# A two-layer hybrid attention and convolution backbone: GpSimd issues the shifted z copies and tap loads, adaLN weights in whole units

## What is computed

```
mod = silu(c) @ w_ada[l] + b_ada[l]          # 1024 x 6144, and the same for c_ctx
sh1, sc1, gt1, sh2, sc2, gt2 = split(mod, 6)
h = rmsnorm(x, g_mix) * (1 + sc1) + sh1      # the context tokens with their own mod
q, k, v, u = split(h @ w_in)                 # 512, 128, 128, 1024 columns
a  = windowed attention (q, k, v), rotary, a sink logit per head
z  = u[:, :512] * sigmoid(u[:, 512:])
cv = silu(layernorm(depthwise_conv31(z) + b_dw))
x += gt1 * (concat(rmsnorm(a), rmsnorm(cv)) @ w_out)
x += gt2 * swiglu(rmsnorm(x, g_ffn) * (1 + sc2) + sh2)
```

## Time and profile before

| | us |
|---|---|
| median of three runs | 1832.35 (1830.58 to 1836.26) |
| the profiled execution | 1837.83 |
| its span, first to last instruction | 1836.0 |

### The profile page before, as it was taken

The page is one execution under the profiler, slowest core; times in us unless marked ns, Lnnn a source line. Parts: engine busy times, 40 slices in busy tenths (PEclk is TensorE's granted clock), DMA queues, the critical chain, the costliest instruction groups (busy, mean ns, idle before and its releaser), DMA issues.

```text
span 1836.0 us, 26721 instructions
## 1 busy us (share of the span) xinstructions
PE 1626.8 (89%) x10540; PEld 1353.1 (74%) x10540; DVE 836.7 (46%) x1530; ACT 634.5 (35%) x1010; POOL 62.6 (3%) x46
## 2 busy tenths in 40 slices
PE   5877976768799999999999998997767899999997
PEld 1654565757678877888788877757755798998995
DVE  2311245878663332343223344227877644344345
ACT  2311115983534321122102223214974453222222
POOL 0000000002320000000000000000003100000000
PEclk9988988998889999999999999899999999999998
DMA  8344342000112134212342234341001232223322
GB/s 338 118 133 123 117 138 92 1 1 24 35 47 67 58 103 160 93 57 73 111 161 69 67 133 144 106 118 58 1 1 48 79 91 92 92 91 92 94 89 81
DMA packets 50147, 165.11 MB, mean 90 GB/s; under 512 B 6928, under 2 KB 7312, under 8 KB 50064
## 3 DMA queue, kind: packets, MB, share of 16 engines
q1 hardware_dynamic: 50064, 163.97, 27.9%
HBM read 150.77 MB, written 2.10 MB: 83 GB/s over the span
## 4 chain that ended last, share of the span: by engine, by line
PE 70%; DVE 7%; issue 7%; ACT 6%; DMA 5%; POOL 2%; SPq 2%; ACTq 0%; DVEq 0%; POOLq 0%
PE banks L446 60%; PE banks L474 4%; POOL x L1325 2%; DMA ada_raw<-in_w_ada 2%; PE banks L404 2%; PE banks L560 1%; DVE probT L1056 1%; ACT probT L735 1%; SPq L334 1%; PE banks L574 1%; ACT prob L718 1%; PE banks L548 1%; DMA ada_early<-in_w_ada 1%; DVE w_low L921 1%; DMA sinT<-in_rope 1%
## 5 line engine op out<-in xcount | busy, mean ns | idle before, releaser
L446 PE MATMUL banks<-h_high,w_high 128*128 128x258 f32 (+2 forms) x2048 | 504.8, 326 | 36.6 <-DVE h_low L950 20.0
L446 PE MATMUL banks<-h_low,w_high 128*128 128x258 f32 (+2 forms) x2048 | 495.2, 321 | 0.0
L446 PE MATMUL banks<-h_high,w_low 128*128 128x258 f32 (+2 forms) x2048 | 494.0, 320 | 0.0
L648 ACT ACTIVATE w_high<-raw 128x1024 fp32r<-128x1024 f32 (+1 forms) x178 | 185.1, 1040 | 741.7 <-PE banks L446 541.8
L446 PEld LDWEIGHTS banks<-h_high,w_high 128*128 128x128 f32 x2048 | 326.7, 194 | 83.3 <-issue 43.2
L921 DVE TENSOR_TENSOR w_low<-raw,w_high 128x1024 fp32r<-128x1024 f32 (+1 forms) x178 | 218.1, 1225 | 328.5 <-ACT w_high L648 325.4
L446 PEld LDWEIGHTS banks<-h_low,w_high 128*128 128x128 f32 x2048 | 326.5, 194 | 28.6 <-issue 0.7
L446 PEld LDWEIGHTS banks<-h_high,w_low 128*128 128x128 f32 x2048 | 325.4, 193 | 27.9
L964 DVE COPY shift_product<-banks 128x2 f32<-128x2 f32 x116 | 18.4, 159 | 450.2 <-PE banks L446 424.6
L446 PE MATMUL banks<-ff_high,w_high 128*128 128x512 f32 (+1 forms) x528 | 164.5, 366 | 0.5 <-DVE ff_low L1259 0.5
L446 PE MATMUL banks<-ff_low,w_high 128*128 128x512 f32 (+1 forms) x528 | 162.3, 362 | 0.0
(11 more groups left out here) (124 smaller groups left out, 1356.6 us busy)
## 6 DMA issues: line engine op xcount, KB each, us to landing
raw<-in_w_gu SPq DMA_DIRECT2D x88, 512.0 KB, 3.5
ada_raw<-in_w_ada SPq DMA_DIRECT2D x80, 512.0 KB, 4.4
raw<-in_w_dn SPq DMA_DIRECT2D x32, 512.0 KB, 3.6
raw<-in_w_mix SPq DMA_DIRECT2D x28, 512.0 KB, 4.6
ada_early<-in_w_ada SPq DMA_DIRECT2D x16, 512.0 KB, 11.0
raw<-in_w_out SPq DMA_DIRECT2D x16, 512.0 KB, 3.6
z_shifted<-z_padded SPq DMA_DIRECT2D x64, 101.4 KB, 4.1
raw<-in_w_dn SPq DMA_DIRECT2D x16, 384.0 KB, 3.1
```

The lines of the kernel that those rows point to most:

```text
L446: last = mm(bank[:, 2 * slot + bk, 0:b - a], weights[w][:, k0_w + k, :], rhs[:, k0_rhs + k, a:b], start=(k == 0 and n == 0), stop=(k == kt ...
L648: f(wH[j][:, 0:k, :], raw[j][:, 0:k, :], ACT.Copy).then_inc(w_high, 1)
```

## The change

GpSimd's program gets the 16 shifted copies of each z tile and the loads of w_conv; SyncE keeps the weights, adaLN, x and the output. GpSimd starts a tile's copies as soon as z and the buffer allow it, and loads the taps of tiles 2 and 3 behind their copies. An adaLN unit is now 128 rows x 2048 columns, 1 MiB, eight per group. Group 0 has seven buffers ada_first over regions that are idle at that time, the eighth unit goes into ada_raw. Later groups alternate between ada_raw and a second place: over the K and Q region in u, over w_conv in qkv (from its second unit on, after the fourth convolution), behind the FFN tiles in dn. In u and dn one unit stands behind each block; in qkv blocks 1 and 3 have two. TensorE computes convolution tiles 0, 1 and 2 behind blocks 5, 6 and 7 of u, and tile 3 behind qkv block 0 as before. ScalarE's conv_copy calls move with them. The arithmetic is the same.

```diff
-AHW = AGW // 2
-ADA_UNITS, EARLY = 2 * DT, 8
...
-        ada_raw = [sb(f"ada_raw{j}", [P, AHW]) for j in range(2)]
-        wD = [sb(f"w_conv{j}", [P, TG, P]) for j in range(2)]
+        ada_raw = sb("ada_raw", [P, AGW])
+        wD = sb("w_conv", [P, 2, TG, P])
+        ada_in_qkv = wD[:].rearrange("p j g m -> p (j g m)")
...
-                s.enter_context(nc.sbuf_tensor("gap_early", [P, CT * (ZW + T)], F32))
-                ada_early = [s.enter_context(nc.sbuf_tensor(f"ada_early{j}", [P, AHW], F32)) for j in range(EARLY)]
+                ada_first = [s.enter_context(nc.sbuf_tensor(f"ada_first{j}", [P, AGW], F32)) for j in range(DT - 1)]
+            with ExitStack() as s:
+                s.enter_context(nc.sbuf_tensor("gap_conv", [P, CT * (ZW + T)], F32))
+                ada_in_u = s.enter_context(nc.sbuf_tensor("ada_in_u", [P, AGW], F32))
+            with ExitStack() as s:
+                s.enter_context(nc.sbuf_tensor("gap_ff", [P, 2 * max(CHUNKS) * T], F32))
+                ada_in_ff = s.enter_context(nc.sbuf_tensor("ada_in_ff", [P, AGW], F32))
...
-            return [(ADA_IN[layer, name], u) for u in range(ADA_UNITS) if u * (blocks - 1) // (ADA_UNITS - 1) == block]
-
-        Z_SHIFTS = {("u", 5): 0, ("u", 7): 1, ("qkv", 0): 2, ("qkv", 1): 3}
-
-        def ada_buffer(i):
-
-            if i < ADA_UNITS:
-                return ada_early[i % EARLY], early_in[i % EARLY], 16 * (i // EARLY + 1)
-            return ada_raw[i % 2], ada_in[i % 2], 16 * ((i - ADA_UNITS) // 2 + 1)
-
+            at = (0, 1, 1, 2, 3, 3, 4, 5) if name == "qkv" else [k * (blocks - 1) // (DT - 1) for k in range(DT)]
+            return [(ADA_IN[layer, name], k) for k in range(DT) if at[k] == block]
...
+        ADA_PLACES, uses, last_use = {}, [0, 0], [DT, DT]
+        for g in range(1, 2 * AG):
+            for k in range(DT):
+                place = k % 2
+                uses[place] += 1
+                second = {ADA_IN[0, "u"]: ada_in_u[:], ADA_IN[0, "qkv"]: ada_in_qkv}.get(g, ada_in_ff[:])
+                tile = second if place else ada_raw[:]
+                ADA_PLACES[g, k] = (tile, ada_in[place], 16 * uses[place], last_use[place])
+                last_use[place] = g * DT + k + 1
+        for k in range(DT):
+            ADA_PLACES[0, k] = (ada_first[k][:] if k < DT - 1 else ada_raw[:], first_in[k], 16, 0)
+
+
+        CONV_AFTER = {("u", 5): 0, ("u", 6): 1, ("u", 7): 2, ("qkv", 0): 3}
...
-                i = unit[0] * ADA_UNITS + unit[1]
-                tile, landed, _ = ada_buffer(i)
-                if EARLY <= i < ADA_UNITS:
-                    sp.wait_ge(ada_mm, i - EARLY + 1)
-                if i >= ADA_UNITS + 2:
-                    sp.wait_ge(ada_mm, i - 1)
-                sp.dma_start(tile[:], w_ada[unit[0], unit[1]]).then_inc(landed, 16)
-
...
+                tile, landed, _, free = ADA_PLACES[unit]
+                if free:
+                    sp.wait_ge(ada_mm, free)
+                if unit == (ADA_IN[0, "qkv"], 1):
+                    sp.wait_ge(conv_mm, CT)
+                sp.dma_start(tile, w_ada[unit[0], unit[1]]).then_inc(landed, 16)
...
+            for j in range(2):
+                sp.dma_start(raw[j][:].rearrange("p k m -> p (k m)"), w_mix[0, j, 0]).then_inc(raw_in[j], 16)
             sp.dma_start(cosT[:], rope[0]).then_inc(const_in, 16)
             sp.dma_start(sinT[:], rope[1]).then_inc(const_in, 16)
...
-                                if (name, 2 * i + j) in Z_SHIFTS:
-                                    shift_z(layer, Z_SHIFTS[name, 2 * i + j])
...
-                        if name == "oa" and layer + 1 < DEPTH:
-                            sp.wait_ge(conv_mm, CT * (layer + 1))
-                            for k in range(2):
-                                load_conv(layer + 1, k)
...
-                    last = mm(bank[32 * q:32 * q + 32, ADA, 256 * half:256 * half + 256], cond[:, k, :],
-                              tile[:, 256 * q:256 * q + 256], start=(k == 0), stop=(k == DT - 1), tile_position=(0, 32 * q))
+                    last = mm(bank[32 * q:32 * q + 32, ADA, :], cond[:, k, :], tile[:, 512 * q:512 * q + 512],
+                              start=(k == 0), stop=(k == DT - 1), tile_position=(0, 32 * q))
...
-                    if name == "u" and i:
-                        conv_tile(layer, i - 1)
+                        if (name, 2 * i + j) in CONV_AFTER:
+                            conv_tile(layer, CONV_AFTER[name, 2 * i + j])
...
                     split_high(layer, "u", i, 0)
+                    if i == 3:
+                        conv_copy(layer, 1, width)
                     split_high(layer, "u", i, 1)
...
-                    if 0 < i < CT - 1:
-                        conv_copy(layer, i - 1, width)
+                    if i == 2:
+                        conv_copy(layer, 0, width)
...
-                conv_copy(layer, CT - 2, width)
-
+
+                conv_copy(layer, 2, width)
...
+            def load_conv(layer, k):
+                pool.dma_start(wD[:, k % 2].rearrange("p g m -> p (g m)"), w_conv[layer, k]).then_inc(wd_in[k % 2], 16)
+
+            def shift_z(layer, k):
+
+                if k == 0:
+                    pool.wait_ge(zpad, layer + 1)
+                pool.wait_ge(z_ok, CT * layer + k + 1)
+                if k >= 2:
+                    pool.wait_ge(conv_mm, CT * layer + k - 1)
+                elif layer == 0:
+                    pool.wait_ge(ada_mm, DT)
+                else:
+                    pool.wait_ge(gemm, 2 * USES[layer, "u"])
+                w = (CC + L if layer == 0 else N) + SH * (TG - 1)
+                for q in range(SH):
+                    for c in range(SH):
+                        pool.dma_start(zr[k % 2][QC * c:QC * c + QC, q, 0:w], z[QC * q:QC * q + QC, k, c:c + w])\
+                            .then_inc(zr_in[k % 2], 16)
...
                 if layer:
                     pool.wait_ge(gemm, 2 * USES[layer, "u"])
+                else:
+                    pool.wait_ge(ada_mm, DT)
                 for a, b in [(0, PAD), (PAD + N, PAD + CC + 2 * layer), (PAD + CC + L, ZW)][:3 - layer]:
                     last = nc.gpsimd.memset(z[:, :, a:b], 0.0)
                 last.then_inc(zpad, 1)
+                if layer:
+                    pool.wait_ge(ada_mm, DT * (ADA_IN[0, "qkv"] + 1))
+                for k in range(2):
+                    load_conv(layer, k)
+                for k in range(CT):
+                    shift_z(layer, k)
+                    if k >= 2:
+                        load_conv(layer, k)
```

More of the change, by code:

```diff
@@ L197, in hybrid_backbone @@
         ada_in = [sem(f"ada_in{j}") for j in range(2)]
-        early_in = [sem(f"ada_early_in{j}") for j in range(EARLY)]
+        first_in = [sem(f"ada_first_in{j}") for j in range(DT)]
         wd_in = [sem(f"w_conv_in{j}") for j in range(2)]
@@ L362, in load_block @@
                                      src[layer, j, i + skip].rearrange("p (k m) -> p k m", m=P)).then_inc(raw_in[j], 16)
-                    if name in ("u", "qkv") or (layer, name) in ADA_IN:
+                    if (layer, name) in ADA_IN:
                         late = []
@@ L397, in ada_unit @@
             def ada_unit(unit):
[L399 to L401 removed]
+                k = unit[1]
+                tile, landed, count, _ = ADA_PLACES[unit]
                 pe.wait_ge(landed, count)
                 for q in range(4):
[L404 to L405 removed]
+                    last = mm(bank[32 * q:32 * q + 32, ADA, :], cond[:, k, :], tile[:, 512 * q:512 * q + 512],
+                              start=(k == 0), stop=(k == DT - 1), tile_position=(0, 32 * q))
                 last.then_inc(ada_mm, 1)
@@ L599, in _ @@
             pe.wait_ge(cond_ok, 1)
-            for u in range(ADA_UNITS - 1):
-                ada_unit((0, u))
+            for k in range(DT - 1):
+                ada_unit((0, k))
             stat_tokens((0, "n1"), TB)
-            ada_unit((0, ADA_UNITS - 1))
+            ada_unit((0, DT - 1))
             pe.wait_ge(const_in, 48)
@@ L620, in _ @@
                             ada_unit(u)
-                        if i + j == 0:
-                            conv_tile(layer, CT - 1)
+                        if ("qkv", 2 * i + j) in CONV_AFTER:
+                            conv_tile(layer, CONV_AFTER["qkv", 2 * i + j])
                 if (layer, "qkv") in ADA_IN:
```

37 lines of the change are left out of this document (7 added, 30 removed).

## The result

The changed kernel takes **1738.1 us** (median of 4 runs, 1736.4 to 1740.2) against 1834.3 for the kernel before (its three runs above and one more): ratio 0.9471, 95% interval 0.9439 to 0.9504. Its profiled execution has a span of 1734.6 us, 101.4 shorter than that of before.

A forecast was written before the change was run, and what follows sets the result against it. Bound: TensorE, 70% its own work, with holes. Gains -3.0 + 57.0 + 4.0 + 14.7 + 5.5 - 2.2 = 76.0 us, so 1832.35 - 76.0 = 1756.4; range 1740 to 1790 (0.83).

The forecast's parts named there:

- the price of a copy on GpSimd: GpSimd's queue, z copies of the convolution tiles: P, GpSimd's time per copy, taken as 1.0 us, 16 copies a tile.
- rival (1): z copies: GpSimd issues as fast as SyncE, P up to 0.85; at 0.7 the kernel takes 1744 us; chance 0.17.
- copies far from 1.0 apart: Sign in GpSimd's queue: copies should stand about 1.0 us apart; far from that, the forecast is wrong.
- 60.7 us of idle and slow time: Layer 0, u and qkv: 181.6 us if nothing waited against 242.3 now; 57.0 of the 60.7 forecast as gain.
- the copies were moving all that time: Layer 0, first convolution tile: 15.8 us from first issue to convolution, 1.0 per copy, so issuing in less would not help.
- Layer 1: From the end of block 1 to the first scores: 122.0 us against 119.8, a loss of 2.2.
- adaLN's own holes: Start of dn0, dn1 and dn2: a 3.39 us hole and slow block each, 4.9 together; gain 14.7 us.
- Rival (5): adaLN: a 1 MiB load outlasts its block, so dn and qkv holes stay; 1789 us; chance 0.03.
- The seam: Layer 0 to layer 1: of the 3.45 and 2.53 us waits, the first goes and some 1.9 stays; gain 5.5 (3 to 7).
- Start: Up to the first product: seven more half units ahead of the last x tile; cost 3.0 us.
- end of qkv: Layer 0, hole between last adaLN unit and transposes: shrinks from 5.8 to some 1.8 us; gain 4.0.
- Rival (4): GpSimd frozen while DVE works: P = 1.0 stretches up to 1.8 in layer 1; 1832 us; chance 0.04.

The follow-up runs named there:

- p10: The kernel after with one GpSimd memset of 128x144 behind every z copy, its end waited for; 1753.2 us.
- ab: The kernel after with the convolution tiles set back one pair, where they stood before; 1746.9 us.
- b_ada: The kernel before with adaLN in whole units over idle regions, SyncE waiting for ada_mm before layer 1's tap loads; 1768.0 us.
- b2: b_ada with SyncE's two tap loads of layer 1 moved ahead of the ob weights instead of the oa weights; 1750.9 us.
- A: Part of the change: GpSimd issues the z copies and tap loads; alone on the kernel before (a_pool) 1805.9 us.
- B: Part of the change: adaLN in whole units over idle regions; alone on the kernel before 1768.0 us (b_ada) or 1750.9 (b2).
- C: Part of the change: the convolution tiles one pair later; alone on the kernel before (c_later) 1803.6 us.
- p1: The kernel after with one GpSimd memset of 128x440 behind every z copy, its end waited for; 1778.6 us.
- p2: The kernel after with three GpSimd memsets of 128x440 behind every z copy; 1897.5 us.
- x_first: The kernel after with all x tiles loaded ahead of adaLN data, own semaphores, token sums and root broadcast between adaLN units 4 and 7; 1728.2 us.
- a_pool: The kernel before with GpSimd issuing the z copies and all tap loads, tiles and adaLN half units unchanged; 1805.9 us.
- bc2: The kernel after with SyncE issuing the z copies and tap loads, layer 1's two tap loads ahead of the ob weights; 1744.3 us.
- c_later: The kernel before with the convolution tiles one pair later and ScalarE's result copies moved to match; 1803.6 us.

## Why the prediction was right or wrong

**Wrong step: the price of a copy on GpSimd.** The argument was that "software has to do what SyncE's queue does in 0.65, and a factor of 1.5 is nearer to that row than one of 3". It takes 0.49, less than SyncE's 0.63. That is rival (1), which had 0.17 and a bound open below 0.85, and it is what the record itself named as its sign of being wrong, copies far from 1.0 apart. p10 shows what hung on it: at P = 1.02 the kernel takes 1753.2, 3 us from the forecast and inside the range. Of the 20 us by which the gain was larger, 15.1 are the price (1753.2 less 1738.1). Put through the recorded sums, P = 0.49 gives about 1740, an estimate: tile 3 of layer 1 is then ready at 65.0 against 64.5, which makes that stretch 109.4 instead of 122.0 (measured 110.0), and the 3.7 of layer 0 go. So the price alone carries the forecast to the lower end of its range, and small gains elsewhere, below, over it. No row excluded a queue cheaper than SyncE's, and no sum was made for one. A slip in rival (1): by its own terms tile 3 of layer 0 is ready at 119.0 against 121.1 at P = 0.7, so the 0.7 charged there is nothing.

**Right number, wrong owner: layer 0.** The forecast added up 60.7 us of idle and slow time and let them go with the copies' new queue, the longer cover and the larger adaLN buffers each taking its own holes. The sum was right (62.8 went: the 3.7 charged for tile 3 did not come, since its copies took 7.8 us instead of 16, and the first block took 10.19 instead of 11.23; the last 1.1 are not placed). The attribution was not. "adaLN and weight loads stood behind 11.6 us of issues" had it the wrong way round: the issues stood behind adaLN waits, 7.3 us late for the first tile. The trace of before had it: ahead of the copies SyncE sends two adaLN loads at 85.66 and a block's weights at 87.55, the former when their buffers are released and not when z is ready. I had read the stream for its length and not for what it waited on.

**Wrong reason: "the copies were moving all that time".** From first issue to use the first tile's copies took 15.8 us in before, and in ab, with GpSimd issuing in 7.8, 93.00 - 77.35 = 15.65. That looks like a limit of the transfer, as the text had it, but b_ada has SyncE's copies landed in 11.8. In before, two adaLN loads and weights had gone out just ahead of the copies. In ab, SyncE sends a 1 MiB adaLN load at 82.63 and weights at 83.95 while GpSimd is still issuing: the first ten copies landed 2.6 to 2.8 us after issue, the last six 3.7 to 8.2, where SyncE's in b_ada took 2.2 to 3.0 with these loads behind them. So the faster issuer made nothing ready earlier there, and the place behind waits is what it cured. In layer 1 it helped a little: from first issue to use 10.96 us in ab against 11.56 in before and 12.64 in b2. That is why A alone left 4.02 of 4.18 at layer 1's first tile, and why it adds so little to B.

By the Trainium skill (DMA: Bandwidth & Descriptors, section Issuing engines are not separate DMA queues), moving transfers to another engine saves only the sequencer's time. The runs agree: beside B, A is worth 4 to 7 us. The prediction set this rule aside because issuing time looked short; what A alone gained, 29 us, it gained because the copies no longer stood behind SyncE's waits.

**Layer 1** was forecast at -2.2 and gave +9.75. The step that failed is again P: with p10's price the stretch takes 121.3, against 122.0 on record. Its gain is accounted for: the first tile's hole and the slow tile after it, 4.18 + 2.73 (9.81 against 7.08 us; the earlier trace rows shows 52 of its 64 matmuls), which is C (ab has it back); the fourth tile's wait, 2.77 to 0.78; the w_low wait before the last block, 1.12 to 0.34.

**adaLN's own holes** went as worked out: no adaLN unit after the first eight waits for a load, and dn0 to dn2 gained 15.7 of 14.7 forecast. In all kernels with B the stretch from the first unit after attention to the last one takes 442.6 to 442.8 us (p1, p2: 440.1), in those without 457.6 to 460.6. Rival (5) is out. The seam gained 7.8 of 3 to 7: the 1.36 that stays of the 2.53 is under the 1.9 foreseen, and the wait of 3.45 is gone. Part of it is not the change's: of the kernels with B, b_ada, b2, after and x_first take 16.3 to 16.4 us for the seam, the others 17.9 to 18.0, and with 17.9 the gain is 6.2, inside the 3 to 7.

**Start** and **end of qkv**: -3.05 and +3.9, as worked out.

**Rival (4)**, GpSimd frozen while VectorE works, is out: the 16 copies take 7.81 to 7.84 us in seven of the eight tiles, while VectorE is busy 39% of layer 0's stretch and 48% of layer 1's. Only layer 1's last tile has a pause of 1.28 behind its ninth copy, and the same in a_pool and ab; its cause stays open.

**Unforecast**: 3.5 us in attention, oa and ob of layer 0. The same instructions took 114.9 to 119.1 us up to the end of attention in the fourteen kernels of this study, with no order that I could tie to the edits. What moves them was not tried.

## What to carry to other kernels

Where an in-order queue issues for several consumers, find for each late transfer which wait stood ahead of it before counting its issues: here a starved two-buffer stream made another stream's transfers 7 us late, and curing it was worth 83 of 96 us, its own holes included. A new wait belongs in a queue with nothing urgent behind it; the same wait ahead of SyncE's weight loads cost 17 us. And when several parts of a change each close the same hole, their gains are alternatives: run them apart before crediting any, and price an unknown term also below the nearest row.

## What was not expected of the hardware

GpSimd issues a strided SBUF copy of 101 KB in 0.50 us and a 512 KB load in 0.57, SyncE the copies in 0.63 to 0.72. The second engine's queue did not bring the data sooner. Copies from issue to landing, in us (the last number): GpSimd's first ten of layer 0's first tile in ab, the five that it issued after SyncE's adaLN load at 82.63, and all 16 from SyncE in b_ada, where that load stands behind them:

```profile
z_shifted<-z_padded POOLq DMA_DIRECT2D x10, 101.4 KB, 2.7
...
z_shifted<-z_padded POOLq DMA_DIRECT2D x5, 101.4 KB, 6.8
...
z_shifted<-z_padded SPq DMA_DIRECT2D x16, 101.4 KB, 2.2
```

In the kernel after, the last of these copies landed 10.5 us after issue.

The same short hole costs clock in one trace and not in another. In all kernels with B the token sums at the seam to layer 1 stand behind a wait of 1.36 to 1.40 us; the work after it, up to the end of block 1, in after and in bc2 (stretch, us, busy times, granted clock, DMA share, GB/s):

```profile
1055.30:1065.80 10.50, 10.47 (x82) 9.94 (x83) 3.44 (x10) 2.28 (x4) 0.00 (x0) 1.00 0.08 25
1057.30:1069.30 12.00, 11.99 (x81) 11.11 (x82) 3.44 (x10) 2.26 (x4) 0.00 (x0) 0.86 0.11 26
```

Holes of 3.3 us do the same. In a_pool's profiled execution the four adaLN holes of 3.3 us in qkv after the first are each followed by a block of 8.69 us at full speed, in the kernel before the same four by blocks of 9.7 to 11.1. The granted clock is 0.99 in a_pool from 51.9 to 255.7 and 0.85 in before from 205.9 to 291.2. Longer holes ahead are not needed for that: in c_later, with none over 3.5 us in layer 0 once the products run, these blocks take 9.8 to 11.1 as well, and at the start of dn0 a_pool's own block after such a hole takes 10.9. So a stretch of some us of difference between two traces can be this alone. What decides it stays open.
